# One attention layer of a long kernel: the scores no longer wait for all the head norms, and two of the norms move in among the units of attention

## The reference, cut to what matters

```python
def _mixer_ab(xn, w_in, w_out, qn_a, kn_a, qn_b, kn_b, rel_bias):
    qa, ka, va, qb, kb, vb = jnp.split(xn @ w_in, [...], axis=-1)
    oa = _moba(_rms(_heads(qa, MOBA_HEADS), qn_a), _rms(_heads(ka, MOBA_HEADS), kn_a), ...)
    ob = _dilated(_rms(_heads(qb, DIL_HEADS), qn_b), _rms(_heads(kb, DIL_HEADS), kn_b), ...)
    ...
    return o @ w_out
```

## Time and profile before

| | us |
|---|---|
| runs shown | 2898.86, 2911.69, 2940.95 |
| their median | 2911.69 |
| the profiled execution: time | 2900.88 |
| its span, first to last instruction | 2898.9 |
| ab's `qknorm` from its first matmul to its last | 2012.8 to 2070.0 |
| ab's attention, to the first matmul of the stage behind it | 2080.96 to 2160.1 |

### The profile page before, as it was taken

The page is one execution under the profiler, slowest core; times in us unless marked ns, Lnnn a source line. Parts: engine busy times, 40 slices in busy tenths (PEclk is TensorE's granted clock), DMA queues, the critical chain, the costliest instruction groups (busy, mean ns, idle before and its releaser), DMA issues. The chain is left out here.

```text
span 2898.9 us, 40646 instructions
## 1 busy us (share of the span) xinstructions
PE 2687.6 (93%) x15617; PEld 2263.1 (78%) x15617; DVE 1563.7 (54%) x2281; ACT 1320.6 (46%) x2001; POOL 22.0 (1%) x34
## 2 busy tenths in 40 slices
PE   6999998998899999899999798997899998889998
PEld 3788786875688877688876657997669997768998
DVE  7444434885644433644323565545757656556655
ACT  6444323464544422544312354544446544445644
POOL 0000000000000000000000000000000001000000
PEclk9999998999999999999999899999999999779999
DMA  6444532201344422344322202544215544302544
GB/s 244 174 159 163 191 138 73 97 20 44 119 170 153 165 102 101 122 168 155 131 90 100 103 1 81 181 174 162 102 59 188 181 178 162 128 11 73 188 174 145
DMA packets 52721, 374.81 MB, mean 129 GB/s; under 512 B 5823, under 2 KB 7035, under 8 KB 8737
## 3 DMA queue, kind: packets, MB, share of 16 engines
q1 hardware_dynamic: 50288, 360.73, 34.7%
q0 software_dynamic: 1920, 12.27, 1.2%
q10 hardware_dynamic: 432, 0.73, 0.1%
HBM read 372.55 MB, written 7.39 MB: 131 GB/s over the span
## 5 line engine op out<-in xcount | busy, mean ns | idle before, releaser
L1092 DVE TENSOR_TENSOR wlo<-raw,whi 128x1024 fp32r<-128x1024 f32 x666 | 799.6, 1222 | 823.0 <-ACT whi L657 821.9
L657 ACT ACTIVATE whi<-raw 128x1024 fp32r<-128x1024 f32 x666 | 684.7, 1053 | 867.6 <-PE acc L1586 781.5
L1584 PE MATMUL acc<-hhi,whi 128*128 128x256 f32 (+1 forms) x2800 | 939.7, 336 | 53.9 <-DVE hlo L1176 36.2
L1585 PE MATMUL acc<-hlo,whi 128*128 128x256 f32 (+1 forms) x2800 | 934.0, 334 | 0.0
L1586 PE MATMUL acc<-hhi,wlo 128*128 128x256 f32 (+1 forms) x2800 | 933.0, 333 | 0.0
L1584 PEld LDWEIGHTS acc<-hhi,whi 128*128 128x128 f32 x2800 | 536.4, 192 | 117.0 <-issue 61.9
L1586 PEld LDWEIGHTS acc<-hhi,wlo 128*128 128x128 f32 x2800 | 536.4, 192 | 50.8
L1585 PEld LDWEIGHTS acc<-hlo,whi 128*128 128x128 f32 x2800 | 536.8, 192 | 48.8 <-issue 0.2
L1584 PE MATMUL acc<-ghi,whi 128*128 128x512 f32 (+1 forms) x1056 | 364.0, 345 | 22.5 <-DVE glo L1249 15.1
L1585 PE MATMUL acc<-glo,whi 128*128 128x512 f32 (+1 forms) x1056 | 362.8, 344 | 0.0
L1586 PE MATMUL acc<-ghi,wlo 128*128 128x512 f32 (+1 forms) x1056 | 362.5, 343 | 0.0
(11 more groups left out here) (245 smaller groups left out, 2584.6 us busy)
## 6 DMA issues: line engine op xcount, KB each, us to landing
raw<-in_slabs SPq DMA_DIRECT2D x333, 1024.0 KB, 4.8
ada_raw<-in_slabs SPq DMA_DIRECT2D x8, 1024.0 KB, 22.8
skew_dram<-lines_dram POOLq DMA_DIRECT2D x1, 6144.0 KB, 24.9
bt<-skew_dram POOLq DMA_DIRECT2D x4, 1024.0 KB, 6.5
x<-in_x_in SPq DMA_DIRECT2D x1, 2048.0 KB, 18.0
out<-x SPq DMA_DIRECT2D x1, 1024.0 KB, 4.8
rope<-in_rope POOLq DMA_DIRECT2D x1, 512.0 KB, 4.0
mask<-in_mask POOLq DMA_DIRECT2D x1, 512.0 KB, 4.7
```

The lines of the kernel that those rows point to most:

```text
L657: nc.scalar.activation(whi[:, n % 2, cols], raw_of(n, cols), ACT.Copy).then_inc(ready, 1)
L1092: nc.vector.tensor_tensor(wlo[:, n % 2, cols], raw_of(n, cols), whi[:, n % 2, cols].bitcast(F32), ALU.subtract).then_inc(low, 1)
L1584: nc.tensor.matmul(out, w[0], xx[0], start=first, stop=False)
L1585: nc.tensor.matmul(out, w[0], xx[1], start=False, stop=False)
```

## The change

Four edits, all for the ab layer alone.

1. VectorE's loop in `qknorm` makes three turns instead of four: the head norms of slabs 0 to 5. The low parts of the two value slabs that stood in the fourth turn follow right behind the loop.
2. The head norms of slabs 6 and 7 are done by a new function, `late_head_norm`, behind biased(4) in turn 1 and behind biased(7) in turn 4 of the attention loop.
3. TensorE no longer waits for `att_ready`. scores(0), (8), (16) and (24) wait for `qk_done` up to the head norm of slab 4, 5, 6 and 7; scores(1) waits for all roots, since it writes bank `B[1]`, in which sums of squares lie.
4. TensorE does scores(0) ahead of the value steps 0 to 7, then scores(1) and (2), then steps 8 to 15. Before it did all 16 steps and then the three scores.

```diff
@@ VectorE, qknorm @@
                 n = st.n0
-                with dve.Fori(0, st.slabs // 2) as i:
+                loops = st.slabs // 2 - (1 if st.slabs == 8 else 0)
+                with dve.Fori(0, loops) as i:
...
-                step.end(2, st.slabs // 2)
+                step.end(2, loops)
+                if st.slabs == 8:
+                    lo(n + 8)
+                    lo(n + 9)
+
+            def late_head_norm(c):
+
+                st = [s for s in plan if s.kind == "qknorm" and s.slabs == 8][0]
+                dve.wait_ge(std_ready, st.std0 + c + 7)
+                step.done(nc.vector.reciprocal(prod[:, c, :], prod[:, c, :]))
+                tiles = QK[:, 12 + 2 * c:14 + 2 * c, :]
+                g = st.gain + 6 + c
+                nc.vector.scalar_tensor_tensor(tiles, tiles, vec[:, g:g + 1],
+                                               prod[:, c, :].rearrange("p (a b) -> p a b", a=2), ALU.mult, ALU.mult)\
+                    .then_inc(qk_done, 1)
@@ VectorE, att @@
                     if u + LEAD < UNITS:
                         biased(u + LEAD)
+                    if st.what == "ab" and u in (1, 4):
+                        late_head_norm(u // 4)
@@ TensorE, att @@
                 x_final(pe, st)
-                pe.wait_ge(att_ready, st.att0 + 1)
                 if st.what != "ab":
+                    pe.wait_ge(att_ready, st.att0 + 1)
...
-                if ab:
-                    for step in range(16):
-                        value_step(0, step)
...
                     pe.wait_ge(s_free, A0 + u + 1)
+                    if ab and u % 8 == 0:
+                        pe.wait_ge(qk_done, 2 + st.qk0 - 3 + u // 8)
+                    if ab and u == 1:
+                        pe.wait_ge(std_ready, st.std0)
...
                 for u in range(LEAD):
                     scores(u)
+                    if ab and u != 1:
+                        for step in range(4 * u, 4 * u + 8):
+                            value_step(0, step)
```

## The result

| | before | changed |
|---|---|---|
| median, us | 2906.8 (22 runs) | 2935.2 (22 runs) |
| lowest and highest | 2898.9 to 2943.9 | 2934.0 to 2938.1 |
| profiled execution: span | 2898.9 | 2932.3 |
| its mean granted clock | 0.953 | 0.936 |

The changed kernel is slower by 28 us in the medians; the ratio is 1.0085, with a 95% interval of 1.0061 to 1.0108.

The account below looks back on a forecast made before the run. TensorE, busy 93% of the span, was taken as the bound, so only its idle time counts. Terms: -11.7 + 6.3 + 2.9 = -2.5 us on a median of 2906.3, forecast 2903.8 us, range 2889 to 2930.

Parts of the forecast that it names:

- The start: From the last sum of squares to ScalarE's value copy: TensorE's wait for att_ready goes, gain 11.7 us.
- The wait for the roots: At scores(1), behind the early start: roots end at 2071.9, scores(1) issues at 2072.8, so it costs nothing.
- rival 4: At attention's start: another wait replaces att_ready; if the start gains only 5 us, 4 us slower than before; chance 0.06.
- The stalls: At turned(2) and turned(5): TensorE waits 3.0 and 3.3 us behind the late head norms, loss 6.3 us.
- Rival 2: In the units: VectorE works ahead and one or both stalls shrink, -8 to -12 us; chance 0.12.
- rival 1: In the units: the clock holds through both stalls, -5.4 us, some 2901; chance 0.20.
- The clock: Behind each of the two stalls: the clock falls once, 1.44 us each, loss 2.9 us.
- My own sign of being wrong: In units 2 to 12: a clock low for more than 12 us would show a term wrong.
- rival 3: Behind the stalls: the clock stays low to turn 12, some 20 us, making the kernel 3.5 us slower, 2910; chance 0.12.

Follow-up runs that it names:

- e3: The changed kernel with 20 extra matmuls on TensorE between scores(3) and turned(0), in its rest ahead of turn 0; 2942.7 us, ratio 1.0110.
- e4: The changed kernel with ScalarE's exps(0) to (2) written ahead of its copy of the first values; 2932.7 us, ratio 1.0073.
- e6: The changed kernel with extra matmuls filling all three rests, ahead of turned(0), turned(2) and turned(5); 2898.4 us against 2901.1 before, ratio 0.9984.
- e12: The changed kernel with late head norms in pieces and 5 extra matmuls ahead of turned(0); 2931.6 us, ratio 1.0082.
- e7: The kernel before plus one pause: VectorE work of some 4.2 us on unread data in turn 1; 2943.3 us, ratio 1.0131.
- e9: The changed kernel with the late head norms cut into pieces, ScalarE's order as it was; 2931.6 us, ratio 1.0083.
- e14: TensorE as in the kernel before, the last two head norms moved into the units in pieces; 2935.2 us, ratio 1.0058.
- e8: The changed kernel with 3 extra matmuls in front of the scores of each unit from 3 on; 2918.4 us, ratio 1.0044.
- e13: The kernel before with 88 extra matmuls in TensorE's wait of 11 us for att_ready; 2942.6 us, ratio 1.0091.
- e1: The kernel before with edits 3 and 4 alone: early start, all eight head norms in front as before; 2935.4 us, ratio 1.0087.
- e2: The kernel before with edits 1 and 2 alone: late head norms, TensorE's wait and order as before; 2946.2 us, ratio 1.0124.
- e5: The changed kernel with exps(0) to (2) ahead of ScalarE's value copy and each late head norm in five pieces; 2891.5 us, ratio 0.9952.
- e11: The kernel before with one short VectorE instruction ahead of normalised(0), to lengthen the rest; two executions at 2904 and 2905 us, two at 2954 and 2956.
- e10: The kernel before with 18 extra matmuls in its rest ahead of turned(0); 2911.5 us against 2910.9, ratio 1.0007.

## Why the prediction was wrong

**The start** was right: 11.2 us measured, 11.7 forecast. The wait for the roots cost nothing, no other wait took its place (rival 4 is out).

**The stalls** were right in place and mechanism. In the changed kernel they are 1.06 and 1.47 us, since at half clock TensorE comes later to turned(2) and turned(5) and VectorE has more time. Entered at full clock the first is 2.76 us (e3, e4) against 3.0 forecast; the second was never seen at full clock. e6, which has start and stalls but no half clock, is the sum of these two terms alone, forecast at -5.4 us: in its profile the way from the last sum of squares to the stage behind attention is 2155.1 - 2068.4 = 86.7 us against 91.3, that is -4.5, and its median is 2.7 us under before (its extra matmuls may take a little longer than the rests that they fill). Rival 2, hidden norms, did not come about. Nor did rival 1; the limit of some 3 us that the prediction quotes in its favour doesn't hold here: rests of 1.60 (e12), 2.38 (e7) and 2.39 us (e9) each dropped the clock.

**The clock is the step that failed**: the term of 2.9 us for two short falls was one fall of 40.5 us. With it the sum is -11.2 + 2.5 + 40.5 = +31.8 where I had -11.7 + 6.3 + 2.9 = -2.5. My own sign of being wrong, a clock low for more than 12 us in units 2 to 12, came true. The step failed in three ways.

First, I priced a fall at 1.44 us, by the 15 slow matmuls of the value block. That block is nothing but matmuls of 128 rows and 256 columns close behind each other, and there the clock came back in 3 us. The units have only six such matmuls each, and from the 25th on none, among scores of 64 rows, transposes and short products, and there it didn't come back in 111 us. The price of a fall in the units is 7.72 - 4.42 = 3.3 us for each pair with value steps, to the end of the stage. Taking the fall alone out of the changed kernel (e6) gives 123.1 - 86.7 = 36.4 us back, less than 40.5, mostly since at full clock the two stalls are longer.

Second, I argued against rival 3 that TensorE "is wholly busy outside the stalls". Being busy was not enough to raise the clock: TensorE was busy, as the profile counts it, for all of 100.90 us in e14 at 0.50, and only with three more dense matmuls a unit (e8) did the clock come back before the stage was over. The row that should have warned me was in my hands, though there TensorE also stood still for 22 us: 49.3 of 71.5 us busy at 0.50 from 2500.5 on the earlier trace rows. I let rival 3 last "to turn 12, some 20 us" for no reason but caution; its rate of loss, 44%, was right (3.3 of 7.72 us is 43%), its end was not.

Third, I looked for the falls behind the two stalls and put nothing at all for the rest ahead of turn 0, as the clock survives the one of 2.15 us in the kernel before. There the fall came. The kernel before survived it in most executions only (89 of 110 beside all runs here lie under 2915 us), and e13 shows that it did so because of the very wait that the change takes away.

That is also why e1 and e2 are each as slow as both together: each takes away most of the wait of 11 us (e2 keeps 2.4 of it), and after that any of the rests that the runs left was enough (1.60 us in e12 the shortest). The wait that cost 11 us also kept the rest behind it harmless; with the rests gone too (e5, e6) the gain stands.

The Trainium skill (TensorE: Matmul & The Clock Gate, "Part 1: The HAM clock gate") says that the full clock comes back once TensorE has been busy for a short while. The dense stages here agree (3.1 us from 2080.96 to 2084.1 in the kernel before); the units of attention do not, and by that rule rival 3 had no case. The measurement decides.

**The range**, to 2930, was made by the scatter of the runs and 4 us of mechanism; with rival 3 carried to the end of the stage it would have had to reach 2940 and more (an estimate: 111.3 us at half clock x 0.44 = 49 lost, 5.4 gained, on 2906.3). The six executions of before at 2940 to 2944, one of which (2940.95) was among the three I had, are what a fall in the units gives (e7 2943.3, e13 2942.6). I called it scatter. No profile of one was taken, but the mean granted clock is on record for the 15 such executions beside e1 to e14: 0.933 to 0.936, as in e7 (0.935 to 0.937), where all others of the kernel before have 0.947 or more. Half the clock for some 105 of 2940 us is 0.018 of the mean, which is the difference; that it fell in this same stage is argued from that size and from the equal times.

**What stays open:** what about the wait of 11 us shields the rest behind it, and why it does so in most executions and not in all. It is neither the size of the rest alone (e11, e12) nor simply that the clock has just come back (in e14 it had, 3.5 us ahead of the rest). e13 is one kernel, and it doesn't separate the fall of the clock in the wait from the idle time itself. Open is too what decides between 71.7, 81.9 and 99.0 us in the later stage; it puts some 12 us of scatter on every comparison here, against effects of 30 and more, and of 9.6 for e5.

**The version that beats both** is e5. It keeps the early start, lets the first softmax run beside the value steps, and does the norms in pieces that fit into the slack: 9.6 us faster than before in the medians (ratio 0.9952, interval 0.9934 to 0.9971) and 43.7 faster than the changed kernel. In its units no rest is above 0.48 us until the last turns, and the clock is full until then:

```profile
2062.00:2139.40 77.40, 74.29 (x436) 53.09 (x435) 54.86 (x184) 43.46 (x118) 0.00 (x0) 1.00 0.21 75
2139.40:2148.20 8.80, 6.19 (x23) 3.52 (x22) 3.75 (x13) 3.30 (x9) 0.00 (x0) 0.50 0.34 119
```

## What to carry to other kernels

Ahead of a stretch of small matmuls and transposes, treat a rest of TensorE, of 1.6 us or more by the runs here, not as that much time but as a bet on the clock for the whole stretch: look for where the clock could come back, and if there is no dense block before the end, price the fall to the end. A few executions that lie one fixed step above the others can be a hint that such a bet is already being lost now and then, and their mean granted clock says whether it is. Work moved onto an engine "with slack" fits only in pieces smaller than the slack of one turn; and matmuls that compute nothing, put into a rest, are a quick test of whether a loss is waiting or clock.

## What the runs showed of the hardware that was not expected

- A granted clock of 0.50 held for 100.90 us in which TensorE was busy for 100.90 (e14). Three more matmuls of 256 columns a unit brought it back after 20.5 us (e8); without them it took the next stage, 4.6 us of dense matmuls (the changed kernel).
- A rest of 1.60 us was enough for the fall in ten of ten executions (e12, one of them profiled); behind one of 2.48 us in the kernel before the clock held in two of four (e11, one of them profiled).
- Filling an idle wait of 11 us with matmuls made the kernel 31 us slower in the medians (2942.6 against 2911.9, e13).
- The kernel before has three times, not two: 2899 to 2907, 2910 to 2915 and 2940 to 2944 us. The second goes with a later attention stage at half clock for 99.0 us (e10's profile, 2914.6 us) in place of 71.7 (the profile before, 2900.9 us). In all 16 profiles that stretch lasts 71.7, 81.9 or 99.0 us.
